# A state space branch in pairs of heads: the past chunks' part in one matmul for both, its decay behind it, and a gate block at the head of each group

## What is computed

```
    a_cs = jnp.cumsum(ac, axis=-1)
    lmat = jnp.exp(jnp.where(tril, seg, -jnp.inf))
    cb = jnp.einsum("bclgn,bcsgn->bgcls", cc, bc)
    y_diag = jnp.einsum("bgrcls,bcsgrp->bclgrp", cb[:, :, None] * lmat, xc)
...
    y_off = jnp.einsum("bclgn,bcgrpn,bgrcl->bclgrp", cc, prev_states, jnp.exp(a_cs))
    y = (y_diag + y_off).reshape(bsz, s, g, r, p) + d_skip.astype(jnp.float32).reshape(g, r)[..., None] * xs.astype(jnp.float32)
...
    return _rmsnorm(y * jax.nn.silu(z), ssm_norm_w)
```

## Time and profile before

| | |
|---|---|
| median of 3 runs | 3093.79 us (3093.28 to 3101.42) |
| profiled execution, its own time | 3090.94 us |
| its span | 3089.6 us |
| mean granted TensorE clock | 0.977 |
| TensorE busy in the span | 2906.8 us, 94% |
| `stage_ssd` in the span | about 1781 to 2058 us |

### The profile page before, as it was taken

One profiled execution on the slowest core, in us unless ns is written; L12 is line 12 of the kernel. 1 busy time (PEld: TensorE's weight loads), 2 busy tenths in 40 slices (PEclk: granted clock), 3 DMA queues, 4 the chain that ended last, 5 costly groups with the idle time before them and its releaser, 6 DMA issues.

```text
span 3089.6 us, 37145 instructions
## 1 busy us (share of the span) xinstructions
PE 2906.8 (94%) x14288; PEld 2336.4 (76%) x14288; DVE 1618.1 (52%) x2859; ACT 1297.5 (42%) x2320; POOL 883.5 (29%) x655
## 2 busy tenths in 40 slices
PE   7998889999999999999997989999999999989987
PEld 6876668777778888887774866678887888877876
DVE  5666774454188888885467665430001444452024
ACT  5255563444266776674434333451112333332122
POOL 1222341123255544542120233223321111103331
PEclk9989999999999999999998999999999999999999
DMA  4400011221100000002112100012211000001231
GB/s 166 168 25 32 26 44 61 79 89 35 44 13 11 12 10 10 13 25 82 50 49 84 48 14 14 18 38 72 72 48 41 28 28 28 28 21 51 72 109 68
DMA packets 54255, 148.84 MB, mean 48 GB/s; under 512 B 5952, under 2 KB 14784, under 8 KB 54080
## 3 DMA queue, kind: packets, MB, share of 16 engines
q1 hardware_dynamic: 54080, 146.46, 14.5%
HBM read 129.66 MB, written 16.78 MB: 47 GB/s over the span
## 4 chain that ended last, share of the span: by engine, by line
PE 82%; DVE 11%; ACT 4%; issue 2%; POOL 1%; DMA 0%; SPq 0%; ACTq 0%; DVEq 0%; POOLq 0%
PE ps L315 78%; PE ps L360 4%; DVE t L792 1%; DVE t L763 1%; PE ps L2310 1%; ACT t L300 1%; DVE t L779 1%; DVE t L1496 0%; DVE t L2547 0%; DVE t L1772 0%; DVE t L2554 0%; DVE t L1675 0%; DVE t L2644 0%; DVE t L1127 0%; ACT t L2397 0%
## 5 line engine op out<-in xcount | busy, mean ns | idle before, releaser
L315 PE MATMUL ps<-t,t 128*128 128x512 f32 (+7 forms) x12400 | 2740.1, 378 | 142.4 <-DVE t L792 23.7
L315 PEld LDWEIGHTS ps<-t,t 128*128 128x128 f32 (+3 forms) x12400 | 2136.0, 186 | 674.6 <-issue 194.7
L306 POOL TENSOR_TENSOR t<-t,t 128x1024 fp32r<-128x1024 f32 (+2 forms) x171 | 359.6, 2103 | 1321.5 <-ACT t L300 1320.9
L300 ACT ACTIVATE t<-t 128x1024 fp32r<-128x1024 f32 (+2 forms) x205 | 186.9, 912 | 719.9 <-PE ps L315 719.7
L1552 POOL TENSOR_SCALAR t<-t,t 128x1024 f32<-128x1024 f32 x128 | 145.3, 1135 | 182.9 <-DVE t L1502 180.0
L360 PE MATMUL ps<-t,t 128*128 128x128 f32 x1176 | 160.5, 274 | 13.2 <-DVE t L1496 7.6
L1496 DVE TENSOR_TENSOR t<-ps,t 128x512 fp32r<-128x512 f32 x256 | 164.3, 682 | 15.7 <-ACT t L1413 13.9
L360 PEld LDWEIGHTS ps<-t,t 128*128 128x128 f32 x1176 | 131.7, 140 | 37.6 <-issue 25.5
L1509 DVE TENSOR_REDUCE t<-ps 128x1 f32<-128x1024 f32 x128 | 154.1, 1204 | 1.9 <-PE ps L315 1.9
L1413 ACT ACTIVATE t<-ps 128x512 fp32r<-128x512 f32 x256 | 140.2, 592 | 11.4 <-PE ps L360 7.2
L1421 ACT ACTIVATE t<-ps,t 128x1024 f32<-128x1024 f32 x128 | 142.8, 1116 | 1.9 <-DVE t L1509 1.5
(11 more groups left out here) (215 smaller groups left out, 2449.1 us busy)
## 6 DMA issues: line engine op xcount, KB each, us to landing
t<-in_wflat SPq DMA_DIRECT2D x156, 512.0 KB, 3.6
t<-in_wada SPq DMA_DIRECT2D x48, 256.0 KB, 4.7
t<-in_xT SPq DMA_DIRECT2D x16, 512.0 KB, 7.5
t<-in_wflat SPq DMA_DIRECT2D x32, 128.0 KB, 2.0
hd<-t SPq DMA_DIRECT2D x8, 512.0 KB, 3.1
t<-hd SPq DMA_DIRECT2D x8, 512.0 KB, 6.5
x2d<-t SPq DMA_DIRECT2D x8, 512.0 KB, 2.7
md<-t SPq DMA_DIRECT2D x16, 256.0 KB, 4.3
```

Of the source, the lines that this page charges most:

```text
L300: ac.activation(whi[i % 2][:, 0:n], raw[i % 2][:, 0:n], ACT.Copy).then_inc(*on.up(ac, "whi", i))
L306: e.tensor_tensor(wlo[i % 2][:, 0:n], raw[i % 2][:, 0:n], whi[i % 2][:, 0:n], ALU.subtract) \
L315: return pe.matmul(o, l, r, start=start, stop=stop)
```

## The change

A pair t of heads (2t and 2t+1) shares one block of 128 rows of XS. The past chunks' part of both is now one matmul for each chunk, with 64 rows and 128 columns of weights (both heads' states, PS) and plain C (CT) moving; it no longer adds up with the own chunk's. The decay is put into the pair's CP buffer, one head in the lower and one in the upper 64 partitions, and VectorE multiplies the result by it afterwards. GpSimd's product of decay and C is gone. The own chunk's matmul is as before, but the odd head writes the upper 64 partitions. VectorE then has three steps for a pair, each for two halves and on 128 partitions (`pair_out`), where it had one for each head on 64. `heads_out` becomes `earlier_chunks` and `own_chunk`; PSUM banks are fixed by use: 0 and 1 past chunks, 2 and 3 own chunk, 4 and 5 segments, 6 and 7 gates. The gate steps of block 4g go to the head of the group, one ahead of the states and one behind them; the first three heads have no gate step, and the last head of each group has two. No gate step is left for the tail.

```
+            slots = {3: [(1, 0)], 4: [(1, 1)], 5: [(2, 0)], 6: [(2, 1)], 7: [(3, 0), (3, 1)],
+                     11: [(5, 0)], 12: [(5, 1)], 13: [(6, 0)], 14: [(6, 1)], 15: [(7, 0), (7, 1)]}
...
+                    gate_pe(4 * g, 0)
                     for c in range(7):
-                        b = sbank["states", g, c] = next_bank(*every)
+                        b = sbank["states", g, c] = next_bank(0, 1, 2, 3)
...
-                    for r in range(8):
-                        if r < 7:
-                            segments(g, r + 1)
-                        heads_out(g, r)
-                        for t, hf in gate_steps[g, r]:
+                    gate_pe(4 * g, 1)
+                    for h in range(8 * g, 8 * g + 8):
+                        if h % 8 < 7:
+                            segments(h + 1)
+                        if h % 2 == 0:
+                            earlier_chunks(h // 2)
+                        own_chunk(h)
+                        for t, hf in slots.get(h, ()):
                             gate_pe(t, hf)
...
-                        o, cols = ps[0:64, b, c * P:(c + 1) * P], slice(cc * P, (cc + 1) * P)
-                        mm(o, XDT[:, cc, 64 * r:64 * r + 64], M[:, cols], True, False)
-                        t = mm(o, PS[rg, cc, 64 * r:64 * r + 64], C[rg, cols], False, True)
...
+            def earlier_chunks(t):
...
+                on.wait_ge(pe, "state", g, 6, 1)
+                for hf in range(2):
+                    wait_bank(hf)
+                    for c in range(4):
+                        cc = 4 * hf + c
+                        x = mm(ps[:, hf, c * P:(c + 1) * P], PS[rg, cc, cols], CT[rg, cc * P:(cc + 1) * P], True, True)
+                    x.then_inc(*on.up(pe, "y earlier", t, hf))
+                    freed[hf] = [("y decayed", t, hf)]
...
+                        x = mm(ps[vr, b, c * P:(c + 1) * P], XDT[:, cc, 64 * r:64 * r + 64], ML[h % 2][:, cc * P:(cc + 1) * P], True, True)
...
+            def pair_out(t):
+                for hf in range(2):
...
+                    on.wait_ge(dv, "decay in", 2 * t + 1, hf)
+                    dv.tensor_tensor(E, ps[:, hf, :], E, ALU.mult).then_inc(*on.up(dv, "y decayed", t, hf))
...
+                    dv.scalar_tensor_tensor(y, y, v("dsk", t), ps[:, 2 + hf, :], ALU.mult, ALU.add).then_inc(*on.up(dv, "y own", t, hf))
...
+                    dv.tensor_tensor(y, y, E, ALU.add).then_inc(*on.up(dv, "y out", t, hf))
...
-                po.tensor_tensor(C[rg, :], C[rg, :], CT[rg, :], ALU.mult).then_inc(*on.up(po, "c decayed", g, r))
```

More of the change, by code:

```diff
@@ L1919, in tensor @@
                         freed[b] = [("cb out", g, c2)]
-                    segments(g, 0)
+                    segments(8 * g)
                     for c in range(8):
-                        b = sbank["xdt", g, c] = next_bank(*every)
+                        b = sbank["xdt", g, c] = next_bank(0, 1, 2, 3, 6, 7)
                         wait_bank(b)
@@ L1942, in tensor, with segments @@
                             gate_pe(t, hf)
-                for t, hf in tail:
-                    gate_pe(t, hf)
                 on.ends(pe, "end ssd", "pe")
             def gate_pe(t, hf):
-                bank[ZS[t], hf] = lin(ZS[t], hf, next_bank(*every), Uh, Ul, need_c, [("zs_silu", "C", t, hf)])
-            def segments(g, r):
+                bank[ZS[t], hf] = lin(ZS[t], hf, next_bank(6, 7), Uh, Ul, need_c, [("zs_silu", "C", t, hf)])
+            def segments(h):
                 for hf in range(2):
-                    b = sbank["seg", g, r, hf] = next_bank(*every)
+                    b = 4 + hf
@@ L2006, in vector @@
                         dv.tensor_tensor(nx, ps[rg, sbank["states", g, c], :], nx, ALU.add).then_inc(*on.up(dv, "state", g, c, 1))
[L2007 to L2017, removed]
+                    for h in range(8 * g, 8 * g + 8):
+                        if h % 8 < 7:
+                            weigh_dv(h + 1)
+                        if h % 2:
+                            pair_out(h // 2)
+                        if h % 8 == 1:
+                            for hf in range(2):
+                                gate_dv(4 * g, hf)
+                        for t, hf in slots.get(h, ()):
                             gate_dv(t, hf)
-                for t, hf in tail:
-                    gate_dv(t, hf)
                 on.ends(dv, "end ssd", "dv")
+            def pair_out(t):
+                for hf in range(2):
+                    y, E = XS[:, t, half(hf)], CP[t % 2][:, half(hf)]
+                    on.wait_ge(dv, "y earlier", t, hf)
+                    on.wait_ge(dv, "decay in", 2 * t + 1, hf)
+                    dv.tensor_tensor(E, ps[:, hf, :], E, ALU.mult).then_inc(*on.up(dv, "y decayed", t, hf))
+                for hf in range(2):
+                    y, E = XS[:, t, half(hf)], CP[t % 2][:, half(hf)]
+                    on.wait_ge(dv, "y", 2 * t + 1, hf)
+                    dv.scalar_tensor_tensor(y, y, v("dsk", t), ps[:, 2 + hf, :], ALU.mult, ALU.add).then_inc(*on.up(dv, "y own", t, hf))
+                for hf in range(2):
+                    y, E = XS[:, t, half(hf)], CP[t % 2][:, half(hf)]
+                    on.wait_ge(dv, "y own", t, hf)
+                    dv.tensor_tensor(y, y, E, ALU.add).then_inc(*on.up(dv, "y out", t, hf))
             def gate_dv(t, hf):
@@ L2054, in scalar @@
                 for g in range(2):
[L2055 to L2059, removed]
+                    weigh_ac(8 * g)
+                    for hf in range(2):
+                        gate_ac(4 * g, hf)
+                    for h in range(8 * g, 8 * g + 8):
+                        if h % 8 < 7:
+                            weigh_ac(h + 1)
+                        if h % 8 == 1:
+                            for hf in range(2):
+                                square(4 * g, hf)
+                        for t, hf in slots.get(h, ()):
                             gate_ac(t, hf)
-                for t, hf in tail:
-                    gate_ac(t, hf)
+                            square(t, hf)
                 on.ends(ac, "end ssd", "ac")
```

115 lines of the change are left out of this document (45 added, 70 removed).

## The result

| | before | change |
|---|---|---|
| median of 4 runs, same chip | 3093.53 us (3092.24 to 3101.42) | 3044.27 us (3042.41 to 3045.37) |
| profiled execution, its own time | 3090.94 us | 3044.63 us |
| its span | 3089.6 us | 3043.3 us |
| mean granted TensorE clock | 0.977 | 0.977 |

The ratio is 0.9834 (0.9822 to 0.9847): faster by 49.3 us in the medians and 46.3 us between the two profiled executions. 3053 was forecast, 40 us faster on the profiled execution.

The account below looks back on a forecast made before the run. TensorE was taken to bound the head loops. 44 and 5 us gained, 9 lost and clock 0 make 40 us, 3051 from the profiled execution or 3054 from the median; 3053 was said, own range 3043 to 3064.

Parts of the forecast that it names:

- TensorE's own work: Head loops: a pair's matmuls and shape changes go from 12.34 to 6.86 us, 44 us gained over 8 pairs.
- ungated heads: Three heads per group without a gate step: TensorE idles 2.9 us in group 0, 5.7 in group 1; 9 us lost.
- heads of the groups: Gate work moved into the waits there leaves 10.5 of 15.6 us of TensorE idle: 5 us gained, bounds 0 and 12.
- clock: TensorE's granted clock: the low stretch at group 1's head goes, a later wait costs the same: 0.
- the block's price: Own-chunk and past-chunk matmuls: 0.36 us each alternating, 0.24 in blocks of one kind, 0.22 per change of shape.
- VectorE's cover: Gated pair: VectorE has 16.4 us of work against TensorE's 21.2, so TensorE sets the pace and `pair_out` costs nothing.
- 24 matmuls at 0.24: A pair's 8 past-chunk and 16 own-chunk matmuls on TensorE, 0.24 us each: 5.76 us.
- the loader's idle of 0.17: Alternating blocks: the weight loader idles 0.17 us a matmul on "issue", taken to come where the shape changes.
- The rival of 3132: VectorE bounds every head if eight steps a pair take 1.8 us more: 78 us more, 3132; chance 0.04.
- the later wait of 5.7: TensorE's wait in group 1's ungated heads, 5.7 us, taken to cost as much in clock as the wait removed.
- the wait at the head of group 1: Before the change: clock at 0.55 of full over 15.16 us behind it, put at 7 us lost.
- The bound that the prediction named: Clock: 7 us more lost if the wait in group 0's ungated heads brings the clock down too.

Follow-up runs that it names:

- grouped: The kernel before, with each head's 16 alternating matmuls in heads_out issued as 8 own-chunk ones and then 8 past-chunk ones: 3056.31 us, ratio 0.9875.
- mixed: The changed kernel, with the even head's 8 own-chunk and the pair's 8 past-chunk matmuls alternating: 3056.89 us, ratio 0.9879.
- pairs: The changed kernel without gate blocks at the heads of the groups, one gate step behind each head from the second on, as before: 3039.15 us, ratio 0.9818.
- moredve: The changed kernel with ten more VectorE steps of 128x512, two in the weighing of each of heads 11 to 15: 3046.64 us, ratio 0.9851.
- later: The changed kernel, with VectorE's gate products of block 4g and ScalarE's squares behind head 3's weighing instead of ahead of it: 3035.82 us, ratio 0.9813.
- gates: The kernel before, with its old `heads_out` but the change's places for the gate steps: 3079.27 us, ratio 0.9951.

## Why the prediction was right, and where its sizes were off

TensorE in the stage, before and after:

```profile
1781.25:2051.90 270.65, 255.03 (x1302) 175.42 (x1302) 139.05 (x260) 100.48 (x135) 83.14 (x39) 0.96 0.06 17
```
```profile
1781.24:2007.10 225.86, 206.59 (x1174) 170.63 (x1174) 145.98 (x276) 93.08 (x129) 36.76 (x23) 0.96 0.07 20
```

The ledger of the stage in the profiled executions, term by term:

| term | predicted | measured |
|---|---|---|
| TensorE's own work | 44 | 45.0 (busy 48.4 less, without the clock's part) |
| ungated heads | -9 | -8.2 |
| heads of the groups | 5 | 4.8 |
| clock | 0 | 3.4 (an estimate, below) |
| sum | 40 | 45.0, of 44.8 in the stage |

Another 1.5 us of the 46.3 between the two executions lie outside the stage, and no term covers them.

The mechanisms came as forecast: the block's price, the waits and their places, VectorE's cover. What was mis-sized is the clock's term, put at 0, and a little of TensorE's own work.

- **TensorE's own work.** The gated pair was put at 21.2 us and takes 20.95, 0.25 less, which for 8 pairs would make 46; the busy time has 45. The mis-sized step is "24 matmuls at 0.24": the 16 own-chunk ones take 0.215. That the loader's idle of 0.17 belonged to the change of shape is shown by `grouped` (gone when the shapes are grouped) and `mixed` (back when they alternate). `grouped` also divides the gain: 38 us (32.5 in the stage) come from the order alone. The step from `grouped` to `pairs`, 17.2 us (18.3 in the stage), is the shared matmul: 64 fewer at 0.215 to 0.24 are 14 to 15, and there are 1.9 us less of idle and 6.8 less at the lower clock (3.4 by the same estimate); together these are 19 to 21, a little more than what was gained. The Trainium skill's rule that the prediction weighed (TensorEngine Tiling (Array Packing), Key Properties: a change of tiling mode drains TensorE, a change of tile does not) holds here: the odd head writes the upper half at the same 0.215. By these runs a change costs 0.15 to 0.17 us.
- **VectorE's cover.** 16.4 us a pair were predicted and 16.4 stand in the timeline. `pair_out` costs 0.68, 0.74 and 0.68 us a step, as taken. The rival of 3132 needed over 1.2 us more in each of eight steps of a pair, and none lengthened but one gate product (1.03 to 1.07); `moredve` shows besides that 2.7 us more a pair cost TensorE nothing. The gate product (minimum, median and longest in ns) has a lower median, where the earlier trace rows had 890:

```profile
L2043 DVE TENSOR_TENSOR t<-t,t x16: 684/689/2501, 1830.3 to 2003.2; 128x512 f32<-128x512 f32 x16
```

  The prediction put the long ones down to GpSimd, whose 45 us of work were to go. The product of C was not what they ran into: every long one, before and after, stands beside a low part of a weight block, which stays (last section).

- **The ungated heads.** 2.9 and 5.7 us of idle were counted, 2.69 and 5.47 stand in the timeline, at the named places and with the named releaser. `later` shows that VectorE's two gate products with their squares make 5.2 of them, as the count had them queued ahead of head 3's weighing. `gates` adds what the count did not ask: without the pairs the same order costs 1.69 us in all.
- **The heads of the groups.** 6.8 and 3.7 us of idle were predicted, 6.0 and 4.8 are there. The gain of 5 was right for the change as it stands, but it is less than the loss of 8.2 that the move brings: the prediction had this sign in its own terms (5 and -9), and `pairs` confirms it with 5.1 (6.0 in the stage).
- **The clock.** This term was the largest miss. I took the later wait of 5.7 to cost what the wait at the head of group 1 had. Time at the lower level, worked out from the windows as twice the share missing from 1.00: before, 6.7, 3.5 and 13.6 us, 23.8; after, 6.9, 3.2, 3.3 and 3.6, 17.0. Half of the difference is 3.4 us, an estimate, as TensorE was not busy in all of it. The bound that the prediction named came true in kind: the wait in group 0 brings the clock down too. But both dips behind the new waits are short:

```profile
1834.95:1838.37 3.42, 3.37 (x15) 2.89 (x15) 2.93 (x9) 1.48 (x3) 0.00 (x0) 0.50 0.00 0
1944.18:1947.59 3.41, 2.94 (x13) 2.94 (x14) 2.22 (x6) 1.64 (x3) 0.00 (x0) 0.50 0.00 0
```

  Why they are short stays open. Alternating blocks stayed at the lower level for long: 13.7 us before, 10.2 in `mixed` behind a wait of 1.46, 10.2 in `gates` behind one of 1.69. But `grouped`, with blocks of one kind behind the same wait as before, was there for 10.2 too, and `pairs`, with the change's blocks, for 3.4 behind a wait of 2.83. These runs also differ in when TensorE waits, so the kind of block is not isolated. The Trainium skill's TensorE: Matmul & The Clock Gate, Part 1, has idleness bring the clock to 1.2 GHz, by which the prediction had 7 more to lose in group 0. The trace agrees in kind, since the clock is at 0.50 soon behind the 2.69 us there, but not in that amount: 3.4 us at half the clock cost some 1.7.

The medians differ by 3 us more than the profiled executions; the median of before lay 2.6 above its profiled run, that of the change 0.4 below.

## What to carry to other kernels

Read the weight loads one by one before shortening a busy TensorE: an idle of the loader that returns after each matmul, with "issue" as its releaser, marks matmuls of two shapes in turn, and putting each shape in a block took 38 of 3094 us (32.5 of them in this stage) for an edit of a few lines. A filler block has a price where it is taken from as well as a gain where it goes, and both depend on how fast the work around it is: the same move was worth 10 us of the stage before the blocks were shortened and cost 6 after. When a stall appears behind such a move, shift the covering block on the waiting engine by one place, which here gave another 11.5 us. Compare such variants by the length of the stage as well, since the medians held up to 6 us that came from elsewhere.

## What the runs showed of the hardware that was not expected

A float32 matmul with 128 moving columns takes 0.215 us with 64 columns of weights in a block of its kind, and 0.36 to 0.39 when its neighbour has another shape. Both count as busy: TensorE's 94% in the profile did not move while 50 us of its work went away.

One VectorE product in the change took 2.45 us instead of 0.69, at the seam of the two groups, beside GpSimd's low part of a weight block:

```profile
1892.53 2.34 POOL L306 TENSOR_TENSOR t<-t,t 128x1024 fp32r<-128x1024 f32 x1 [10.95 <-ACT t L300]
1892.96 2.45 DVE L2043 TENSOR_TENSOR t<-t,t 128x512 f32<-128x512 f32 x1 [3.73 <-ACT t L2090]
```

It started 0.43 us after GpSimd's and ended 0.54 after it by these lines, which is what a wait for the whole of GpSimd's instruction would look like; the masks of group 1 stand behind it, and TensorE's wait of 2.21 us for them follows. It is no single case. Six of the change's 16 gate products start beside such a product of GpSimd, and all six end 0.55 us behind it, whatever is left of it: 2.45 and 2.50 us long where it has just begun, 1.03 to 1.07 where it is nearly done, as beside the following one (the gate product is the last line of VectorE's timeline above, 1881.06):

```profile
1879.20 2.38 POOL L306 TENSOR_TENSOR t<-t,t 128x1024 fp32r<-128x1024 f32 x1 [18.59 <-ACT t L300]
```

The other ten, alone, take 0.68 to 0.69. Before, eight of 16 stood so and again ended 0.55 us behind, which made the median of 890 ns; none of them stood beside GpSimd's product of C. The Trainium skill's SBUF — State Buffer, Terms, has the lock between these two engines that would do this. No run here took GpSimd's instruction away, so the cause is read and not tested.
